# Attention's values spread between units, and half of the query stacking moved into the attention

## The reference

```python
def attend(q, k, v, scale):
    s = jnp.einsum('bqhgd,bshd->bhgqs', q, k).astype(jnp.float32) * scale
    p = jax.nn.softmax(s, axis=-1).astype(v.dtype)
    return jnp.einsum('bhgqs,bshd->bqhgd', p, v)
```

## Time and profile before

| what | us |
|---|---|
| three runs | 1542.63, 1538.18, 1542.36 (median 1542.36) |
| the profiled execution | 1539.78, its span 1538.0 |
| busy in the span: PE, DVE, ACT, POOL | 1337.5, 1007.3, 805.0, 438.0 |
| first attention | from 288 to 387: PE busy 74.1 of 99, DVE 65.2, POOL 49.8 |
| second attention | from 997 to 1104: PE busy 89.3 of 107, DVE 66.0, POOL 49.9 |

### The profile page before, as it was taken

One profiled execution on the slowest core, in us unless ns is written; L12 is line 12 of the kernel. 1 busy time (PEld: TensorE's weight loads), 2 busy tenths in 40 slices (PEclk: granted clock), 3 DMA queues, 4 the chain that ended last, 5 costly groups with the idle time before them and its releaser, 6 DMA issues. The chain is left out here.

```text
span 1538.0 us, 17799 instructions
## 1 busy us (share of the span) xinstructions
PE 1337.5 (87%) x6717; PEld 933.7 (61%) x6717; DVE 1007.3 (65%) x1355; ACT 805.0 (52%) x1126; POOL 438.0 (28%) x264
## 2 busy tenths in 40 slices
PE   5989999677792999999989999988697499999995
PEld 1756567454681666666658877555376366666663
DVE  1536415765646888888866338566554688888875
ACT  3612116533422777777755277544322377777772
POOL 0002007554002044444330032355101024444430
PEclk7999999798995999999989999999798599999997
DMA  9578840300517999999951120040231999999954
GB/s 366 224 287 315 325 156 8 150 29 28 218 72 275 348 360 382 381 381 379 368 159 19 59 59 5 8 198 1 92 151 60 372 343 383 380 376 376 379 179 170
DMA packets 63598, 339.11 MB, mean 220 GB/s; under 512 B 16724, under 2 KB 21464, under 8 KB 45080
## 3 DMA queue, kind: packets, MB, share of 16 engines
q1 hardware_dynamic: 57464, 317.31, 54.1%
q0 software_dynamic: 6048, 20.65, 5.7%
HBM read 314.04 MB, written 23.89 MB: 220 GB/s over the span
## 5 line engine op out<-in xcount | busy, mean ns | idle before, releaser
L1696 POOL TENSOR_TENSOR modrow<-modrow,proj 80x1024 f32<-80x1024 f32 x30 | 132.6, 4420 | 311.2 <-ACT modrow L1814 311.2
L1846 DVE TENSOR_TENSOR wlow<-wraw,proj_rounded 128x2048 fp32r<-128x2048 f32 x96 | 217.0, 2288 | 5.3 <-ACT proj_rounded L1788 5.3
L1725 PE MATMUL psum<-wlow,proj_rounded 128*80 128x512 f32 x512 | 202.7, 396 | 0.0
L1788 ACT ACTIVATE proj_rounded<-wraw 128x2048 fp32r<-128x2048 f32 x96 | 180.0, 1909 | 9.2 <-PEq L1377 9.2
L1724 PE MATMUL psum<-proj_rounded 128*80 128x512 f32 x376 | 151.3, 402 | 2.1 <-DVE proj_rounded L1851 2.1
L1726 PE MATMUL psum<-proj_rounded 128*80 128x512 f32 x376 | 148.2, 394 | 0.0
L1304 POOL TENSOR_SCALAR ring<-ring,small 128x640 f32<-128x640 f32 x64 | 99.7, 1563 | 109.1 <-DVE small L1261 108.6
L1287 ACT ACTIVATE ring<-psum,small 128x640 f32<-128x640 f32 (+1 forms) x80 | 56.7, 709 | 100.1 <-DVE small L1255 100.1
L1846 DVE TENSOR_TENSOR wlow<-wraw,xr_rounded 128x2048 fp32r<-128x2048 f32 x32 | 73.3, 2291 | 43.7 <-ACT xr_rounded L1788 43.7
L1725 PEld LDWEIGHTS psum<-wlow,proj_rounded 128*80 128x80 f32 x512 | 76.8, 150 | 39.8 <-issue 1.2
L1725 PE MATMUL psum<-wlow,small_rounded 128*80 128x512 f32 x256 | 100.8, 394 | 0.0
(11 more groups left out here) (469 smaller groups left out, 3251.2 us busy)
## 6 DMA issues: line engine op xcount, KB each, us to landing
wraw<-in_exp_w_gate_dram SPq DMA_DIRECT2D x32, 2048.0 KB, 13.2
wraw<-in_exp_w_up_dram SPq DMA_DIRECT2D x32, 2048.0 KB, 12.6
wraw<-in_exp_w_down_dram SPq DMA_DIRECT2D x32, 2048.0 KB, 13.9
ring<-in_ada_w_dram SPq DMA_DIRECT2D x29, 1024.0 KB, 6.5
hold<-in_ada_w_dram SPq DMA_DIRECT2D x14, 1024.0 KB, 6.4
ring<-in_ev_w_in_dram SPq DMA_DIRECT2D x4, 2048.0 KB, 11.9
xr<-x_rows SPq DMA_DIRECT2D x15, 512.0 KB, 6.9
ring<-in_od_w_in_dram SPq DMA_DIRECT2D x3, 2048.0 KB, 17.0
```

The costliest lines, as they stand in the source:

```text
L1696: pool.tensor_tensor(ye[0:CAP, :], ye[0:CAP, :], g2[0:CAP, :], ALU.mult).then_inc(s["ye"], 1)
L1725: pe.matmul(dst, xs[:, 0, k, :], wl, start=False, stop=False)
L1788: act.activation(high_of(m, h), raw_of(m, h), ACT.Copy).then_inc(s["high"], 1)
L1846: dve.tensor_tensor(low_of(m, h), raw_of(m, h), high_of(m, h), ALU.subtract).then_inc(s["low"], 1)
```

## The change

1. `values(pair, j)` does one key tile j of a pair, or with j = 5 the context's matmuls. It is called behind the turn of units 11 to 16, 21 to 26 and 31 to 36. The last pair's six calls stand behind the loop as before. The take moves from units 14, 24, 34 to units 18, 28, 38.
2. In `mlstm`, GpSimd makes the halves of all keys and of the queries of heads 0 to 3. The queries of heads 4 to 7 are made one head at a time by `later_queries` in the first attention, ahead of GpSimd's units 0, 5, 10 and 15; TensorE waits for them at the first unit of heads 4 to 7.

```diff
-                    for g in range(2):
-                        key_halves(g)
-                        query_halves(g)
+                    key_halves(0)
+                    halves.link(pool.tensor_copy(q_pair[0:64, 0:4], qT[0:64]))
+                    halves.link(pool.tensor_tensor(q_pair[64:P, 0:4], qT[0:64], q_pair[0:64, 0:4], ALU.subtract))
+                    key_halves(1)
...
+                    def values(pair, j):
+                        if j == 0:
+                            pe.wait_ge(s["c0"], TILES * (2 * pair + 2))
+                            if pair >= 1:
+                                pe.wait_ge(s["out"], 2 * pair)
                         for r in range(2):
                             h = 2 * pair + r
+                            if j < TILES:
+                                pe.matmul(psum[64 * r:64 * r + 64, 6, :], v_of(h, 0, j), slots[h % NSL][:, j, :], start=(j == 0), stop=(j == TILES - 1))
+                            else:
+                                mm = pe.matmul(psum[64 * r:64 * r + 64, 7, 0:P], v_of(h, PT, 0), ctxT[:, h % 4, :], start=True, stop=True)
+                        if j == TILES:
+                            mm.then_inc(s["o"], 1)
...
+                            if "gpsimd" in extra and t == 0 and h >= 4:
+                                pe.wait_ge(s["halves"], 2 * (h - 3))
...
-                            if u % (2 * TILES) == 1 and u > 1:
-                                values(u // (2 * TILES) - 1)
-                    values(heads // 2 - 1)
+                            pair, j = u // (2 * TILES) - 1, u % (2 * TILES) - 1
+                            if pair >= 0 and 0 <= j <= TILES:
+                                values(pair, j)
+                    for j in range(TILES + 1):
+                        values(heads // 2 - 1, j)
...
-                            if u % (2 * TILES) == 4 and u > 4:
+                            if u % (2 * TILES) == 8 and u > 8:
                                 take(u // (2 * TILES) - 1)
...
                     for u in range(N):
+                        if "gpsimd" in extra and u % TILES == 0 and u // TILES < 4:
+                            if u:
+                                pool.wait_ge(s["n"], u - (u + TILES - 4) // TILES)
+                            extra["gpsimd"](pool, halves, u // TILES)
...
+        def later_queries(pool, halves, j):
+            halves.link(pool.tensor_copy(q_pair[64:P, 4 + j], qT[64:P, j]))
+            halves.link(pool.tensor_tensor(q_pair[0:64, 4 + j], qT[64:P, j], q_pair[64:P, 4 + j], ALU.subtract))
```

More of the change, by code:

```diff
@@ L1149, in attention @@
         def attention(name, heads, scale, q_of, k_of, v_of, slots, tmp, extra=None, short=0):
-            s = {n: sem(f"{name}_{n}") for n in ("s", "max", "p", "sum", "n", "na", "t", "c0", "o", "out", "own")}
+            s = {n: sem(f"{name}_{n}") for n in ("s", "max", "p", "sum", "n", "na", "t", "c0", "o", "out", "own", "halves")}
             extra = extra or {}
@@ L1201, in turn @@
                         mm.then_inc(s["t"], 1)
[L1203 to L1212, removed]
+                    def values(pair, j):
[3 more added lines that the diff above has]
+                                pe.wait_ge(s["out"], 2 * pair)
                         for r in range(2):
                             h = 2 * pair + r
-                            mm = pe.matmul(psum[64 * r:64 * r + 64, 7, 0:P], v_of(h, PT, 0), ctxT[:, h % 4, :], start=True, stop=True)
-                        mm.then_inc(s["o"], 1)
+                            if j < TILES:
[4 more added lines that the diff above has]
+                            mm.then_inc(s["o"], 1)
                     for i in range(N + NB - 1):
@@ L1296, in _ @@
                     if "gpsimd" in extra:
-                        extra["gpsimd"](pool)
+                        halves = Steps(pool, s["halves"])
                     for u in range(N):
+                        if "gpsimd" in extra and u % TILES == 0 and u // TILES < 4:
+                            if u:
+                                pool.wait_ge(s["n"], u - (u + TILES - 4) // TILES)
+                            extra["gpsimd"](pool, halves, u // TILES)
                         if by_act(u):
@@ L2572, in build @@
         attention("gqa", BH, BD ** -0.5, lambda h, t: q_pair[:, h, t * P:(t + 1) * P],
-                  even_keys, even_values, slots, Carve(ringf, 5 * 4096), extra={"sync": out_loads(0, A["ev_w_out"][0], early)}, short=P)
+                  even_keys, even_values, slots, Carve(ringf, 5 * 4096), extra={"sync": out_loads(0, A["ev_w_out"][0], early), "gpsimd": later_queries}, short=P)
         ready = expert_semaphores(0)
```

## The result

The whole change took 1528.88 us (median of six runs, 1526.99 to 1532.8) against 1539.74 of before in the same six rounds. The ratio is 0.9933 with a 95% interval of 0.9913 to 0.9953, so between 7 and 13 us were won. On a second occasion the ratio was 0.9927 (0.9912 to 0.9942). The profiled execution took 1532.19 us, its span is 1530.4 against 1538.0. The forecast was -10.0 us and 1531.

The account below looks back on a forecast made before the run. A ring of waits, no single full engine, was taken to set the attentions' pace; -3.9 + 2.4 - 4.3 - 2.0 - 1.1 - 1.1 = -10.0 us from 1540.7 gave 1531, range 1522 to 1540.

Parts of the forecast that it names:

- Part A: mLSTM's tail: without the queries of heads 4 to 7, VectorE's stalled product takes 0.35 us again; -3.9 us.
- Part B: First attention: the moved query work on GpSimd delays units 5 and 10 by 1.2 us each; +2.4 us.
- Part C: Both attentions: values spread over six units shorten each pair of heads; -4.3 us in the first, -2.0 in the second.
- a visit: TensorE's switch to a piece of values and back, priced beyond its 0.87 us at 0.33 first attention, 0.20 second.
- B (free): Rival: visits to values cost nothing extra, so spreading gives 13 us instead of 6.3; 1524 us, chance 0.18.
- C (0.55): Rival: each visit costs about 0.55 us extra, losing 8.6 of the 10 us won; 1539 us, chance 0.21.
- D (0.80): Rival: each visit on TensorE costs the full 0.80 us extra, so the kernel is slower; 1547 us, chance 0.09.
- tails of 0.33: Second attention: if changing tiling mode drains TensorE, each visit pays 0.33 us, losing 2.0 us, the spread's whole gain.
- Part D: Last take of each attention moves from unit 34 to 38, where VectorE waits anyway; saves 0.7 and 0.4, -1.1 us.
- Part E: Attentions' half-clock stretches, estimated at 2.2 us for both: shorter TensorE gaps save half, -1.1 us; bounds -3 and +2.
- the signs named in advance: Among signs in the attentions: VectorE's longest wait for scores falls from 4.6 to under 1 us; each shortens about 3.
- the ring: Attention's cycle of waits among TensorE, VectorE and GpSimd; asks 4.5 us for two units, 2.25 each.

Follow-up runs that it names:

- casts: Kernel before, with GpSimd's last subtraction at mLSTM's end replaced by three casts of the same 64x2560; 1541.91 us, one run.
- memsets: Kernel before, with GpSimd's last subtraction at mLSTM's end replaced by three memsets over 64x2560 elements; 1536.55 us, one run.

## Why the prediction was right, step by step

- **Part A, -3.9: right.** The longest product fell from 4.29 to 0.35 us, and the stretch behind the reciprocal from 14.83 to 11.11 (-3.7). That GpSimd's reading holds VectorE's products is shown by casts and memsets. That nothing else was late next held.
- **Part B, +2.4: right as priced, incomplete.** Turn 4 to turn 5 went from 1.20 to 2.30 us and turn 9 to turn 10 from 1.19 to 2.32, 2.2 in sum; units 0 and 15 hid theirs. No VectorE instruction stretched beside the subtractions. What the step left out is the clock: the gaps that it puts into TensorE's queue bring two stretches at half clock, 1.0 and 1.5 us, 2.5 in all. So the queries' move, A and B together, was forecast at -1.5 and is worth about +1 in the rows: the gain of the whole change comes from the values.
- **Part C, -4.3 and -2.0: right.** The pitch with values was 2.34 and 2.83 us, forecast 2.35 and 2.82; the pair of heads 20.56 and 22.8 to 23.0, forecast 20.6 and 23.0; the pair without the take 19.82, forecast 19.8. So a visit costs 0.33 and 0.20 us, and rivals B (free), C (0.55) and D (0.80) are out on that term. The estimate by which tails of 0.33 would take the second attention's gain away did not hold: its visit stayed 0.2. Whether TensorE drains at a visit no run shows.
- **Part D, -1.1: right.** The kernel with only the values has no inner stretch in either attention. Its three pairs from unit 9 to 39 take 19.82, 20.56 and 20.54 us, 60.9 in sum, against three times the 22.0 of before at full clock: 5.1 less, where Parts C and D had 4.3 + 0.7. In the second attention it is 68.3 against three times 23.6 (the pairs of before without a stretch take 23.67 and, in its two variants with casts and memsets, 23.57), 2.5 less, where they had 2.0 + 0.4. Nothing parts C from D in these sums. The take at unit 38 was not the best place: 0.8 us more is won in each attention at units 16, 26 and 36.
- **Part E, -1.1: a guess whose sign came out by luck.** What Parts B, C and D leave of the two attentions' -1.9 and -5.7 is the clock: +1.0 in the first and -3.2 in the second, -2.2 in sum. In the first the inner stretches went from one to two, and what they cost from 1.0 to 2.5 us, where the forecast had 0.5 saved. In the second the inner stretch is gone: all four profiles with values in blocks have one there, which costs 1.6 us, and none of the eight with spread values has. The rest lies at the attentions' ends, where it differs between executions: in the second profile of the whole change the same remainder is about 0 and -5.5. So one profile of each can't settle Part E's size.

The sum -10.0 stands against -10.9 measured, between -7 and -13. That is less good an agreement than it looks. The interval is 6 us wide, two executions differ by 1 to 2 us in stretches that the change does not touch, and two errors cancel in the profiled pair: with Part E halved between the attentions, the first attention's clock came out 1.5 us worse than forecast, by the stretches behind the gaps, and the second's 2.6 better. Rival D's price was not met; the cost that the forecast missed lies at the turns of units 5 and 10, where no rival had looked.

Two of the signs named in advance came out only in part. VectorE's longest wait for scores behind the spread values is 0.97 us in the first attention but 1.46 in the second, and 1.87 behind a stretch at half clock (before 4.62 and 5.11). The attentions shortened by 1.9 and 5.7 us, not by 3 each.

Of the parts taken alone, the queries were forecast at -1.5 and are at no gain (ratio 1.0017): the two stretches behind the gaps at units 5 and 10. The values were forecast at -7 to -8 and are at 0.9943, about -9 and between -6 and -12: as forecast.

## What to carry to other kernels

Work that is moved off one critical place should be put where the receiving engine is not itself followed by a waiting TensorE: the same 2.4 us cost nothing ahead of units 0, 15 and 25 and about 1.1 us each, and a stretch at half clock of 1.0 to 1.5 more, ahead of units 5 and 10. A block in an in-order queue that starves the ring around it can be cut into pieces as fine as the ring's own units, if the switch is cheaper than the idle time (here 0.33 and 0.20 us a visit); with pieces twice as large the ring was longer again. Read the switch's price from the block's entry and exit. Before a two-operand VectorE instruction on the path, look for GpSimd reading SBUF.

## What the runs showed of the hardware

A GpSimd memset leaves VectorE's two-operand products alone, while a GpSimd cast with a single SBUF input holds them back to its end (2.32 us each, against products of 0.35). The trace of before had only shown the subtraction, with two inputs.

TensorE idling for 1.2 to 1.6 us ahead of units 5 and 10 was followed by 3.4 us at the 1.2 GHz level in eleven of eleven cases. Idle time of the same length elsewhere is not followed by one each time, and the same code differs from one execution to the next. In the first attention of the kernel before, TensorE idles 1.47 to 1.56 us ahead of units 16, 26 and 36. The kernel before has its inner stretch at unit 16 (326.0) and none at unit 26:

```profile
349.12 0.74 PE L1200 MATMUL psum<-ident,ring 128*128 128x128 f32 x5 [1.55 <-DVE proj L1269]
```

The kernel with the casts, whose attention is the same, has none at unit 16 and one at unit 26 (from 350.1):

```profile
349.45 0.75 PE L1205 MATMUL psum<-ident,ring 128*128 128x128 f32 x5 [1.56 <-DVE proj L1274]
```

The kernel with the memsets has none before 371.9. So such idle time is what the lower level was seen to follow, but it doesn't decide it alone, and a stretch in one profile is no property of the kernel. What else decides stays open; it was not tried.
